# Local-attention heads by chunks: 8 items of 4 chunks and 2 heads in place of 16 items, with another plan of steps

## What is computed

```
def swa_sink_attention(q, k, v, sinks, cos, sin):      # 8 query heads, 2 key/value heads, 64 wide
    q = apply_rope(...); k = apply_rope(...)
    q = q.reshape(bsz, nc, CHUNK, SWA_KV_HEADS, SWA_GROUP, HEAD_DIM)      # CHUNK = 64
...
    kb = concatenate([previous chunk of k, this chunk of k])              # 128 keys for 64 queries
    vb = concatenate([previous chunk of v, this chunk of v])
    s = einsum('bnqhgd,bnkhd->bnhgqk', q, kb) * (HEAD_DIM ** -0.5)
    s = where(valid, s, NEG)                                              # chunk 0 has no previous chunk
    p = softmax(concatenate([s, sink], axis=-1), axis=-1)[..., :-1]
    o = einsum('bnhgqk,bnkhd->bnqhgd', p, vb)
```

## Time and profile before

| | us |
|---|---|
| median of 3 runs | 1937.14 (1935.67 to 1938.83) |
| the profiled execution, whole | 1934.37 |
| its span, first to last instruction | 1932.6 |
| loop of steps, layer 0, first `scores` to last `attend` | 443.3 to 563.0 |
| loop of steps, layer 1 | 1395.8 to 1515 |
| `glu` starts, layer 0 / layer 1 | 513.38 / 1465.03 |

### The profile page before, as it was taken

How to read it: one execution, slowest core, us unless ns; L and a number is a source line. 1 busy time by engine, 2 the same in 40 slices (tenths; PEclk the granted TensorE clock), 3 DMA queues, 4 the chain that set the end, 5 groups by cost and what they waited for, 6 DMA issues and landing times.

```text
span 1932.6 us, 24716 instructions
## 1 busy us (share of the span) xinstructions
PE 1903.2 (98%) x9114; PEld 1540.7 (80%) x9114; DVE 1007.2 (52%) x1429; ACT 724.5 (37%) x1144; POOL 207.2 (11%) x433
## 2 busy tenths in 40 slices
PE   8999999999999999999999999999999999999998
PEld 6888888877667888888878888887876778888887
DVE  5664432387757544433376544335877574444323
ACT  4332332255654433332243333223656453333221
POOL 2831000023100000000056010000131000000000
PEclk9999999999999999999999999999999999999999
DMA  6334343352212333343333433333512223333331
GB/s 179 109 104 129 97 120 96 87 147 69 66 37 84 102 94 97 98 120 91 97 93 97 142 100 110 106 90 103 153 34 66 66 77 98 98 98 110 105 90 44
DMA packets 330953, 188.53 MB, mean 98 GB/s; under 512 B 6996, under 2 KB 325432, under 8 KB 329848
## 3 DMA queue, kind: packets, MB, share of 16 engines
q1 hardware_dynamic: 324008, 168.13, 30.4%
q0 software_dynamic: 5824, 18.79, 3.4%
q10 hardware_dynamic: 1040, 0.52, 0.1%
HBM read 175.72 MB, written 11.67 MB: 97 GB/s over the span
## 4 chain that ended last, share of the span: by engine, by line
PE 94%; ACT 2%; DVE 2%; DMA 1%; issue 1%; POOL 0%; SPq 0%; DVEq 0%; ACTq 0%; POOLq 0%
PE ps L560 18%; PE ps L562 18%; PE ps L561 18%; PE ps L691 8%; PE ps L690 8%; PE ps L692 8%; PE ps L588 2%; PE ps L589 2%; PE ps L593 2%; PE ps L898 1%; PE ps L875 1%; PE ps L856 1%; DMA raw<-in_ffn_gate 1%; PE ps L848 0%; PE ps L818 0%
## 5 line engine op out<-in xcount | busy, mean ns | idle before, releaser
L1500 DVE TENSOR_TENSOR wl<-raw,wh 128x1024 fp32r<-128x1024 f32 (+1 forms) x265 | 350.5, 1323 | 753.4 <-ACT wh L1047 752.2
L560 PE MATMUL ps<-xh,wh 128*128 128x512 f32 x1552 | 611.9, 394 | 1.2 <-DVE wl L1500 1.2
L562 PE MATMUL ps<-xh,wl 128*128 128x512 f32 x1552 | 605.3, 390 | 0.0
L561 PE MATMUL ps<-xl,wh 128*128 128x512 f32 x1552 | 604.9, 390 | 0.0
L1047 ACT ACTIVATE wh<-raw 128x1024 fp32r<-128x1024 f32 (+1 forms) x265 | 301.1, 1137 | 653.3 <-PE ps L692 341.9
L560 PEld LDWEIGHTS ps<-xh,wh 128*128 128x128 f32 x1552 | 291.8, 188 | 66.4 <-issue 4.2
L562 PEld LDWEIGHTS ps<-xh,wl 128*128 128x128 f32 x1552 | 291.5, 188 | 60.9
L561 PEld LDWEIGHTS ps<-xl,wh 128*128 128x128 f32 x1552 | 291.7, 188 | 59.8 <-issue 1.2
L690 PE MATMUL ps<-Hh,wh 128*128 128x512 f32 x704 | 274.3, 390 | 0.0
L692 PE MATMUL ps<-Hh,wl 128*128 128x512 f32 x704 | 274.2, 390 | 0.0
L691 PE MATMUL ps<-Hl,wh 128*128 128x512 f32 x704 | 274.2, 389 | 0.0
(11 more groups left out here) (329 smaller groups left out, 1800.6 us busy)
## 6 DMA issues: line engine op xcount, KB each, us to landing
raw<-in_ffn_up SPq DMA_DIRECT2D x88, 512.0 KB, 3.8
raw<-in_ffn_down SPq DMA_DIRECT2D x64, 704.0 KB, 4.5
raw<-in_ffn_gate SPq DMA_DIRECT2D x87, 512.0 KB, 3.8
raw<-in_w_in SPq DMA_DIRECT2D x28, 512.0 KB, 4.7
raw<-in_w_out SPq DMA_DIRECT2D x16, 512.0 KB, 4.0
xrow<-in_x SPq DMA_DIRECT2D x2, 1024.0 KB, 8.6
ssm_t<-evict POOLq DMA_DIRECT2D x8, 256.0 KB, 3.2
ssm_v<-evict POOLq DMA_DIRECT2D x8, 256.0 KB, 2.7
```

What stands on the lines that cost most here:

```text
L560: pe.matmul(bank, w_tile(True, slot, kw), xh[:, kx, :], start=first, stop=False)
L561: pe.matmul(bank, w_tile(True, slot, kw), xl[:, kx, :], start=False, stop=False)
L562: return pe.matmul(bank, w_tile(False, slot, kw), xh[:, kx, :], start=False, stop=last)
L1500: V.tensor_tensor(w_low(slot, k0, nk), raw[:, slot4, 0:nk - k0, :], w_high(slot, k0, nk).bitcast(F32), ALU.subtract).then_inc(w_split, 1)
```

## The change

Local items are now 8 a layer: 4 head pairs by 2 groups of 4 chunks. A chunk is 64 queries by exactly its 128 keys (its own chunk and the one before; chunk 0 takes keys 0 to 127 with a mask). The two heads of a pair lie in one tile: head 0's 64 queries on PSUM partitions 0 to 63, head 1's on 64 to 127; a group of 4 chunks fills one bank of 512 columns.

- `scores`: per chunk and head a matmul with 64 contracted rows, 64 columns of weights and 128 moving columns (8 an item), and one bf16 mask product of 128 columns for items with group 0 only. No padded keys, no row masks: POOL's `memset`s of `kz` and `mk` go.
- `maxes`, `exps`, `norms`: one maximum over 4 x 128, one minimum with the sink per partition; four exponentials of 128 columns with their sums, one of the sinks (128x4); one multiply of 128x512 with the reciprocals broadcast.
- `turn`: 4 transposes, each of which holds both heads. `turned`: always 512 columns.
- `attend`: once for every local item, 8 matmuls of 128 contracted rows, 64 weight columns (values) and 64 moving columns.
- Odd chunks take their values from `va`; even chunks need 128 tokens that start in the middle of a block, so `shifted_values` makes three more transposes of the value tile into bank 2, and ACT copies them to `kz[:, 2, :]`. `scores(0)` waits for this copy, since it writes bank 2.
- The plan of steps is shorter (24 items, not 32). `ssm_out` stays at step 4; the GELU halves are at DVE's steps 5 and 8, `glu` at 13. Projection halves 9 to 12 are both in steps 0, 2, 4 and 6 (the second behind `turn`), 13 in steps 9 and 10, 14 in 12 and 14. The column tiles `qc0` and `kc0` change places. The 33 filler products inside the loop go; the 18 behind each post-norm stay.
- The sinks are loaded by two small DMAs at the start, not one.

```
-ITEMS = [("swa", j, None, i, list(range(max(0, i - 1), i + 1))) for j in range(SWA_PAIRS) for i in range(TOK)]
+ITEMS = [("swa", j, None, g, None) for j in range(SWA_PAIRS) for g in range(GROUPS_OF_CHUNKS)]
...
+                        if n == 0:
+                            pe.wait_ge(vs_rdy, l + 1)
...
+                        for cc, c in chunks_of(i):
+                            k0 = keys_from(c)
+                            for a in range(2):
+                                r = slice(64 * a, 64 * a + 64)
+                                mm = pe.matmul(bank[r, cc * P:(cc + 1) * P], qa[r, j, c * CHUNK:(c + 1) * CHUNK],
+                                               kz[r, j // 2, k0:k0 + P], start=(c > 0), stop=True, skip_group_check=True)
...
+                        for cc, c in chunks_of(i):
+                            cols = slice((j // 2) * HD, (j // 2 + 1) * HD)
+                            v = va[:, c // 2, cols] if c % 2 or c == 0 else view_shifted(c // 2 - 1)[:, cols]
                             for a in range(2):
-                                mm = part(n + a, a, b, b)
+                                mm = pe.matmul(ps[PV_BANK][64 * a:64 * a + 64, c * CHUNK:(c + 1) * CHUNK], v,
+                                               probT[:, n % 2, cc * P + a * CHUNK:cc * P + (a + 1) * CHUNK],
+                                               start=True, stop=True, skip_group_check=True)
+                        mm.then_inc(pv_mm, 1)
...
-                    pe.wait_ge(s_exp, l * N_ITEMS + SWA_PAIRS * TOK)
...
-                    if s in SPIN_AT:
-                        spin(BU_BANK[0], SPIN_AT[s])
-                    if s in SPIN_PV:
-                        spin(GLU_BANK[1], SPIN_PV[s])
-                    if s > LAG_PV and (s - LAG_PV) % 2:
-                        attend(s - LAG_PV - 1)
-                    if s in SPIN_TURN:
-                        spin(GLU_BANK[1], SPIN_TURN[s])
+                    m = s - LAG_PV
+                    if 0 <= m < N_SWA:
+                        attend(m)
+                    elif m > N_SWA and m % 2:
+                        attend(m - 1)
                     if LAG_T <= s < N_ITEMS + LAG_T:
                         turn(s - LAG_T)
+                    if s in SECOND_BEHIND:
+                        project_half(SECOND_BEHIND[s], 1)
...
+                        for cc, _ in chunks_of(i):
+                            act.activation(prob[:, b, cc * P:(cc + 1) * P], ps[S_BANK[n % 2]][:, cc * P:(cc + 1) * P], ACT.Exp,
+                                           bias=stat[:, b, cc:cc + 1], accum_out=stat[:, b, 4 + cc:5 + cc]).then_inc(act_c, 1)
+                        act.activation(stat[:, b, 8:12], stat[:, b, 0:4], ACT.Exp, bias=sinks[:, l, j:j + 1]).then_inc(s_exp, 1)
...
-GELU_AT = (7, 11)
-GLU_AT = 17
+GELU_AT = (5, 8)
+GLU_AT = 13
...
-PROJECT_AT = {0: 9, 4: 10, 8: 11, 12: 12, 16: 13, 20: 14}
-SECOND_AT = {1: 9, 5: 10, 9: 11, 13: 12, 17: 13, 23: 14}
...
-SPIN_TURN, SPIN_SUM, SPIN_PV = {21: 3, 22: 3, 24: 3}, {22: 4}, {21: 4, 25: 4}
+PROJECT_AT = {0: 9, 2: 10, 4: 11, 6: 12, 9: 13, 12: 14}
+SECOND_BEHIND = {0: 9, 2: 10, 4: 11, 6: 12}
+SECOND_AT = {10: 13, 14: 14}
+DONE_AT = {1: 9, 3: 10, 5: 11, 7: 12, 11: 13, 15: 14}
```

More of the change, by code:

```diff
@@ L143, in n_first, with chunks_of, keys_from @@
     return 5 if s % 3 == 1 else 4
-def by_rows(n):
-    return ROWS_FROM <= n < SWA_PAIRS * TOK
 def last_item(pr):
-    return (pr + 1) * TOK if pr < SWA_PAIRS else SWA_PAIRS * TOK + (pr - SWA_PAIRS + 1) * 2 * TOK
+    return (pr + 1) * GROUPS_OF_CHUNKS if pr < SWA_PAIRS else N_SWA + (pr - SWA_PAIRS + 1) * 2 * TOK
+def chunks_of(g):
+    return [(cc, ITEM_CHUNKS * g + cc) for cc in range(ITEM_CHUNKS)]
+def keys_from(c):
+    return CHUNK * max(0, c - 1)
 K_ID, K_CAUSAL, K_SWA, K_COS, K_SIN = 0, 128, 256, 512, 1024
@@ L784, in values, with shifted_values @@
                     mm.then_inc(vt_mm, 1)
+                def shifted_values():
+                    pe.wait_ge(f_x, l + 1)
+                    for t in range(TOK - 1):
+                        mm = pe.transpose(ps[VS_BANK][:, t * P:(t + 1) * P], vT[:, CHUNK + t * P:CHUNK + (t + 1) * P], ident[:, :])
+                    mm.then_inc(vs_mm, 1)
                 def ssm_in():
@@ L871, in turn @@
                         pe.wait_ge(v_rdy, l * 3 + 1)
-                    c = 0
-                    for a in range(2 if kind == "swa" else 1):
-                        for b in range(len(keys)):
-                            mm = pe.transpose(ps[PT_BANK][:, c * P:(c + 1) * P],
-                                              prob[:, n % PROBS, a * 2 * P + b * P:a * 2 * P + (b + 1) * P], ident[:, :])
-                            c += 1
+                    for c in range(ITEM_CHUNKS if kind == "swa" else len(keys)):
+                        mm = pe.transpose(ps[PT_BANK][:, c * P:(c + 1) * P], prob[:, n % PROBS, c * P:(c + 1) * P], ident[:, :])
                     mm.then_inc(pt_mm, 1)
@@ L1230, in values @@
                     act.activation(view2(dst), ps[VT_BANK[v]][:, :], ACT.Copy).then_inc(v_rdy, 1)
+                    if v == 0:
+                        act.wait_ge(vs_mm, l + 1)
+                        act.activation(kz[:, 2, 0:(TOK - 1) * P], ps[VS_BANK][:, 0:(TOK - 1) * P], ACT.Copy).then_inc(vs_rdy, 1)
                 def forget():
@@ L1279, in turned @@
                     if n >= 2:
-                        act.wait_ge(pv_mm, g - n % 2)
-                    w = len(keys) * P * (2 if kind == "swa" else 1)
+                        act.wait_ge(pv_mm, g - (1 if n < N_SWA + 2 else n % 2))
+                    w = ITEM_CHUNKS * P if kind == "swa" else len(keys) * P
                     act.activation(probT[:, n % 2, 0:w], ps[PT_BANK][:, 0:w], ACT.Copy).then_inc(pt_rdy, 1)
@@ L2003, in _ @@
                            allow_slow_non_contiguous=True).then_inc(s_small, 16)
-            pool.dma_start(sinks[:, :, :].rearrange("p l h -> p (l h)"),
-                           swa_sinks.rearrange("l h -> (l h)").unsqueeze(0).to_broadcast([P, DEPTH * SWA_HEADS]))\
-                .then_inc(s_small, 16)
+            for a in range(2):
+                pool.dma_start(sinks[64 * a:64 * a + 64, :, :].rearrange("p l j -> p (l j)"),
+                               swa_sinks.rearrange("l (j a) -> a (l j)", a=2)[a].unsqueeze(0).to_broadcast([64, DEPTH * SWA_PAIRS]),
+                               allow_slow_non_contiguous=True).then_inc(s_small, 16)
             n = [1]
```

168 lines of the change are left out of this document (57 added, 111 removed).

## The result

The changed kernel takes 1959.96 us (median of 4 runs, 1958.41 to 1962.94), the kernel before 1936.91 beside it on the same chip: 1.012 times, 95% interval 1.0102 to 1.0137. It is 23 us **slower**. The forecast was 1929.5 with a range of 1914 to 1941, so the time lies outside the range and on the other side. The profiled execution has a span of 1956.6, 24.0 over the one before.

A forecast was written before the change was run, and what follows sets the result against it. TensorE's own work bounds the kernel (94% of the last-ending chain). Saving 14.5 us a layer, less 9 returning as waits and 1.7 for the clock, gives 7.6 over both: 1937.1 to 1929.5, range 1923 to 1934, with neighbours 1914 to 1941.

The forecast's parts named there:

- The POOL memsets, the sink DMAs and the padded keys were waited for by nobody on TensorE: 0.: Start and loop: removing or changing these saves or costs TensorE nothing, 0 us.
- TensorE's work saved: Loop: cheaper scores, transposes, `attend` and less filler, minus 0.3 for shifted values, save 14.5 us a layer, 29 for both.
- saved 5.4: Loop: 33 filler products a layer at 0.16 us each go, counted as TensorE work saved, 5.4 us a layer.
- The walk of waits: Layer 0's loop step by step on three engines: 9 us come back as waits, so it gains 5.5, not 14.5.
- so I count 1.7 a layer: Wait at `glu`: TensorE's clock falls to 1.2 GHz for a time, losing 1.7 us of work a layer.
- the clock stays low: Loop from `glu` to about step 19: 1.2 GHz loses 9 us against 5.5 gained, 3.5 slower a layer, 1944; chance 0.13.
- Small matmuls that overlap badly: Scores before `glu`: 3 to 6.8 us a layer come back, gain near 0, 1934 to 1939; chance 0.17.
- the waits don't come: Loop at and behind `glu`: waits mostly absent, both layers gain 10 to 12 us, 1914 to 1917; chance 0.22.
- The slower side: Whole kernel: slower than before by over 0.2% (3.9 us); chance 0.16, summed from 0.02, 0.02 and 0.12.

The follow-up runs named there:

- `Hh` repaired: Changed kernel with the pad tile four floats smaller (`PAD` 216, not 220), so `Hh` begins at byte 138368 as in the kernel before: 1944.44 us, 1.0038 of before.
- `glu` later and no filler: Changed kernel with contiguous sink load and `Hh` at its old byte, TensorE's `glu` issued one step later, no filler in the loop: 1923.29 us, 0.9939 of before.
- both repairs: Changed kernel with the sinks loaded by one contiguous broadcast and `Hh` back at byte 138368: 1935.32 us, 1.0002 of the kernel before.
- sinks repaired: Changed kernel with the sinks loaded by one contiguous broadcast and laid out by two DVE copies, all else at its byte: 1952.70 us, 1.0094 of before.

## Why the prediction was wrong, point by point

- **"The POOL memsets, the sink DMAs and the padded keys were waited for by nobody on TensorE: 0."** This step failed for the sink DMAs: 8.5 us in the trace, 7.3 to 8.3 in three pairs of runs. It was true of the load that was removed, and was carried over to the two that took its place. At the start TensorE does not wait for their data; but the 16 DMA engines are shared, and the first gate weights stood behind them (they landed at 17.6 us instead of 9.8; in the kernel with `Hh` repaired the `ident` load too, at 16.7 instead of 9.3). The earlier trace rows showed TensorE waiting for a load in this stretch already.
- **What was not a step: the rest of the program stays as it is.** 14.0 us of the loss in the trace, 15.5 in the runs. The diff's `PAD` and the resized tiles were read as bookkeeping, and no row of before could have priced them. They could have been named as unpriced: a change to the sizes of tiles moves every tile behind them, and TensorE's 2112 matmuls of the down-projection read two of these. A bound of 3% of them, 14 us, would have put the upper end nearer to the time, though still under it.
- **TensorE's work saved.** Right term by term: scores 1.02 (1.05), `attend` 0.62 (0.6). Of the 29 us of both layers 22.5 show as less busy time where the clock is nearly full (1880.7, `glu` later and no filler, against 1903.2); in the changed kernel only 3.6 did, since the slower down-projection and the low clock are busy time too.
- **The filler: "saved 5.4."** Right as work, and of the wrong kind. It stood in waits, so taking it out gave nothing, and it held the clock. Taken out of the kernel before, it costs 19.6 us in all, 13.8 of them traced, with 30.6 us at the low level; put into the waits of the repaired kernel it brings 10.0.
- **The walk of waits.** Right. At full clock, with filler in the waits, the loop gains 6.3 and 5.2 us (118.0 and 118.2 against 124.3 and 123.4), 5.5 forecast, and it is 113.1 and 113.4 us long to the last `attend`, 113.9 forecast. In the changed kernel's layer 0 `glu` starts 71.1 after the loop's start, forecast 71.4, though of two parts that missed: DVE's multiply ended 59.5 after it (57.9), and the stores and the load took 11.6 (13.5). The waits were 1.2, 2.56 and 4.24 (1.3, 2.5, 6).
- **The clock: "so I count 1.7 a layer."** Mis-sized: 10.0 us for both layers by the medians, 11.2 by the ratios, so 5 to 5.6 each. The price was taken from one idle stretch in the start, and one fall was counted, at the longest wait. There were two in layer 0 and three in layer 1, 27.2 us at the low level in all, also at the waits of 2.56 and 2.1. The rival "the clock stays low" had its mechanism right (no filler, then a row of waits) and put its turning point at 5.5 us a layer; the runs gave 5 to 5.6. That is why both repairs together come out at no difference.
- **The rivals.** Small matmuls that overlap badly: excluded by 1.02 for 16. That the waits don't come: excluded. The slower side was given 0.16, 0.12 of it for the clock; the two causes that decided stood in none of the cases.

## What to carry to other kernels

When a diff changes the size of any tile, list where the tiles behind it go, and keep the matmul's moving operand and its weights at a distance that was free here (0, 256 or 512 bytes beyond a multiple of 1024; 32, 64 and 128 were not, and no other was measured); every small DMA that changes its form is to be priced by what stands behind it in the engines, not by who waits for its data. Work taken out of an engine that also waits is worth what the waits leave: look at the clock behind every wait, put filler or, better, independent work into it, and look at the clock in both layers of a loop.

## What the runs showed of the hardware

- A 128 x 128 by 512 matmul in fp32r takes 0.2267 us from start to start when weights and moving operand are 0, 256 or 512 bytes apart beyond a multiple of 1024, 0.2333 at 32 and 128, and 0.2289 in the mean at 64. Moving both alike by 32 bytes changes nothing (1935.13 against 1935.06).
- Two loads of 64 partitions by 8 single 4-byte values, 4 KB in all, kept the DMA engines from moving nearly anything else for 8 us at the start: 32 packets of 128 bytes, 3.9 us each. Issued at 28 us, with no other load due, they took 7.8 and 10.7 us to land and cost the kernel nothing that its median shows.
- The clock fell from 2.4 to 1.2 GHz at idle waits of TensorE of 2.4 and 2.56 us too, not only at those of 4, and in two kernels behind one of 1.9. It does not fall every time: at the 2.56 us wait for `qa` it fell in layer 1 alone (the changed kernel and both repairs), in layer 0 alone (sinks repaired), in both (`Hh` repaired) and in neither (`glu` later, no filler). One layer's profile, or one kernel's, isn't enough.
- 33 matmuls a layer whose result nobody reads are worth 19.6 us of 1935 in the kernel before.
